# Strassen's scheme in a down projection: more row tile pairs in it, and its sums spread over two engines

## The reference, cut to what matters

```python
h = rms_norm(x, ln_mix_w)
u_pool, q, f, i, g, gate_a, gate_b = split(h @ w_in)             # 2048 x 9216
y_a = multiscale_pool(u_pool) @ w_branch_a                        # 1024 x 2048
y_b = hgrn2(q, f, i, g) @ w_branch_b                              # the recurrence, 1024 x 2048
x = x + (sigmoid(gate_a) * y_a + sigmoid(gate_b) * y_b) @ w_out   # 2048 x 2048
u = conv3(rms_norm(x, ln_ffn_w) @ w_up)                           # 2048 x 11008
x = x + (silu(u_gate) * u_val) @ w_down                           # 5504 x 2048
x = x + sigmoid(rms_norm(x, ln_ple_w) @ w_ple_gate) * (p @ w_ple)
return rms_norm(x, ln_final_w)
```

## Time and profile before

| | us |
|---|---|
| three runs | 1438.47, 1438.48, 4224.24; median 1438.48 |
| the profiled execution's own time | 1438.39 |
| its span in the profile | 1436.6 |
| TensorE busy | 1425.5 (99%), 7112 matmuls |
| VectorE busy | 985.1 (69%) |
| ScalarE busy | 760.0 (53%) |
| GpSimd busy | 216.9 (15%) |
| granted TensorE clock, mean | 0.999 of full |

### The profile page before, as it was taken

How to read it: one execution, slowest core, us unless ns; L and a number is a source line. 1 busy time by engine, 2 the same in 40 slices (tenths; PEclk the granted TensorE clock), 3 DMA queues, 4 the chain that set the end, 5 groups by cost and what they waited for, 6 DMA issues and landing times.

```text
span 1436.6 us, 19705 instructions
## 1 busy us (share of the span) xinstructions
PE 1425.5 (99%) x7112; PEld 1212.1 (84%) x7112; DVE 985.1 (69%) x1180; ACT 760.0 (53%) x920; POOL 216.9 (15%) x153
## 2 busy tenths in 40 slices
PE   9999999999999999999999999999999999999997
PEld 7888888888888888888888888888888888888886
DVE  7576777845455455566777777777777887787755
ACT  7555655544444444555555555555555546554544
POOL 0044144100000000000101101111011531140000
PEclk9999999999999999999999999999999999999999
DMA  9765555456666655465666566565665656565653
GB/s 325 225 205 161 165 176 159 143 194 190 191 190 191 191 190 188 158 208 181 190 188 191 180 198 186 179 204 175 191 193 177 212 192 200 177 213 188 227 200 121
DMA packets 190875, 273.47 MB, mean 190 GB/s; under 512 B 11744, under 2 KB 103136, under 8 KB 190688
## 3 DMA queue, kind: packets, MB, share of 16 engines
q1 hardware_dynamic: 190384, 272.30, 59.6%
q10 hardware_dynamic: 432, 0.37, 0.1%
HBM read 270.53 MB, written 2.10 MB: 190 GB/s over the span
## 4 chain that ended last, share of the span: by engine, by line
PE 98%; DVE 1%; issue 1%; ACT 0%; ACTq 0%; POOLq 0%; POOL 0%; DVEq 0%
PE main L622 15%; PE main L624 15%; PE main L623 15%; PE aux L747 11%; PE main L747 11%; PE aux L756 6%; PE main L756 6%; PE main L672 3%; PE main L670 3%; PE main L671 3%; PE aux L670 3%; PE aux L672 3%; PE aux L671 3%; PE aux L788 1%; PE aux L818 1%
## 5 line engine op out<-in xcount | busy, mean ns | idle before, releaser
L1301 DVE TENSOR_TENSOR w_lo<-raw,w_hi 128x1024 fp32r<-128x1024 f32 (+1 forms) x490 | 612.4, 1260 | 394.5 <-ACT w_hi L1009 394.3
L1009 ACT ACTIVATE w_hi<-raw 128x1024 fp32r<-128x1024 f32 (+1 forms) x490 | 514.1, 1052 | 541.2 <-PE main L624 284.8
L622 PE MATMUL main<-w_hi,xT 128*128 128x512 f32 x702 | 276.8, 394 | 0.0
L624 PE MATMUL main<-w_hi,xT 128*128 128x512 f32 x702 | 273.6, 390 | 0.0
L623 PE MATMUL main<-w_lo,xT 128*128 128x512 f32 x702 | 273.6, 390 | 0.0
L747 PE MATMUL aux<-xT,w_hi 128*128 128x512 f32 x704 | 169.9, 391 | 0.0
L747 PE MATMUL main<-xT,w_hi 128*128 128x512 f32 x672 | 163.0, 391 | 0.0
L624 PEld LDWEIGHTS main<-w_hi,xT 128*128 128x128 f32 x702 | 131.9, 188 | 27.4
L622 PEld LDWEIGHTS main<-w_hi,xT 128*128 128x128 f32 x702 | 132.0, 188 | 27.0 <-issue 0.4
L623 PEld LDWEIGHTS main<-w_lo,xT 128*128 128x128 f32 x702 | 132.0, 188 | 26.1
L747 PEld LDWEIGHTS aux<-xT,w_hi 128*128 128x128 f32 x704 | 129.4, 188 | 25.2 <-issue 0.3
(11 more groups left out here) (270 smaller groups left out, 1770.7 us busy)
## 6 DMA issues: line engine op xcount, KB each, us to landing
raw<-in_w_up SPq DMA_DIRECT2D x336, 256.0 KB
raw<-in_w_in SPq DMA_DIRECT2D x136, 512.0 KB
raw<-in_w_down SPq DMA_DIRECT2D x84, 512.0 KB
raw<-in_w_out SPq DMA_DIRECT2D x32, 512.0 KB
raw<-in_w_ple_gate SPq DMA_DIRECT2D x32, 512.0 KB
raw<-in_w_branch_a SPq DMA_DIRECT2D x16, 512.0 KB
raw<-in_w_branch_b SPq DMA_DIRECT2D x16, 512.0 KB
raw<-in_w_in SPq DMA_DIRECT2D x15, 256.0 KB, 5.7
```

The lines of the kernel that those rows point to most:

```text
L622: pe.matmul(acc, th, wh, start=first, stop=False)
L624: return pe.matmul(acc, tl, wh, start=False, stop=end)
L1009: ac.activation(w_hi[:, u % RING, :, 0:w], raw[:, u % RING, :, 0:w], ACT.Copy).then_inc(hi_full, 1)
L1301: dve.tensor_tensor(w_lo[:, u % RING, :, 0:w], raw[:, u % RING, :, 0:w], w_hi[:, u % RING, :, 0:w].bitcast(F32), ALU.subtract).then_inc(lo ...
```

## The change

More pairs in Strassen's scheme (seven in each half instead of five), the weight sums 2 and 3 on GpSimd instead of VectorE, the four short activation sums on VectorE instead of GpSimd, two buffers for the high and low activation sums, the x transposes of the down stage one unit later with the splits behind them one slot later, and the transpose of the second recurrence output two units later.

```diff
-OBT = [PV[g] + 4 for g in range(2)]
+OBT = [PV[g] + 4 + 2 * g for g in range(2)]
...
-SEVEN_AT = ((5, 8, 11, 14, 17), (5, 8, 11, 14, 17))
+SEVEN_AT = ((5, 7, 9, 11, 13, 15, 17), (5, 7, 9, 11, 13, 15, 17))
...
-X2_AT = {down_slot(n) + 1: n for n in range(NQ)}
+X2_AT = {down_slot(n) + 2: n for n in range(NQ)}
...
-        a_sums_hi = sb("a_sums_hi", [P, 4, P], F32R, ffn)
-        a_sums_lo = sb("a_sums_lo", [P, 4, P], F32R, ffn)
+        a_sums_hi = sb("a_sums_hi", [P, 2, 4, P], F32R, ffn)
+        a_sums_lo = sb("a_sums_lo", [P, 2, 4, P], F32R, ffn)
...
# SyncE, before a load into a buffer of a Strassen pair
-                    sp.wait_ge(w_summed, 3 * (SEVEN[u - RING] + 1))
+                    sp.wait_ge(w_summed, 2 * (SEVEN[u - RING] + 1))
...
# ScalarE, sums_hi
-                    if q:
-                        ac.wait_ge(w_sums_done, 2 * q)
+                    if q > 1:
+                        ac.wait_ge(w_sums_done, 2 * (q - 1))
...
-                    ac.wait_ge(w_summed, 3 * q + (1, 3)[half])
+                    ac.wait_ge(w_summed if half else w_diffs, 2 * (q + 1) if half else q + 1)
...
# ScalarE and VectorE, high and low parts of x after its transposes (norm is 2 in the down stage)
-                        if s == at + 2:
+                        if s == at + 1 + norm:
...
# VectorE, slot u - 2
-            def weight_sums(u):
+            def weight_diffs(u):
                 q, a, b = SEVEN[u], u % RING, u % RING + 1
-                dve.tensor_tensor(w_sums[:, 0:2, :], raw[:, b, 0:2, :], raw[:, a:b + 1, 0, :], ALU.subtract).then_inc(w_summed, 1)
-                dve.wait_ge(w_summed, 3 * q + 1)
-                dve.tensor_tensor(w_sums[:, 2, :], raw[:, b, 1, :], w_sums[:, 0, :], ALU.subtract).then_inc(w_summed, 1)
-                dve.wait_ge(w_summed, 3 * q + 2)
-                dve.tensor_tensor(w_sums[:, 3, :], raw[:, a, 1, :], w_sums[:, 2, :], ALU.subtract).then_inc(w_summed, 1)
+                if q:
+                    dve.wait_ge(w_sums_ready, 2 * q)
+                dve.tensor_tensor(w_sums[:, 0:2, :], raw[:, b, 0:2, :], raw[:, a:b + 1, 0, :], ALU.subtract).then_inc(w_diffs, 1)
+
+            def act_sums(q):
+                dve.wait_ge(a_joined, q + 1)
+                a = a_sums[:].rearrange("p k (b t) -> p k b t", t=P)
+                a11, a12, a21, a22 = a[:, 0, 0], a[:, 1, 0], a[:, 0, 1], a[:, 1, 1]
+                dve.tensor_tensor(a22, a21, a22, ALU.add).then_inc(a_sum_part, 1)
+                dve.wait_ge(a_sum_part, 3 * q + 1)
+                dve.tensor_tensor(a21, a11, a21, ALU.subtract).then_inc(a_sum_part, 1)
+                dve.wait_ge(a_sum_part, 3 * q + 2)
+                dve.tensor_tensor(a11, a22, a11, ALU.subtract).then_inc(a_sum_part, 1)
+                dve.wait_ge(a_sum_part, 3 * q + 3)
+                dve.tensor_tensor(a12, a12, a11, ALU.subtract).then_inc(a_summed, 1)
...
                 if s + 2 in SEVEN:
-                    weight_sums(s + 2)
+                    weight_diffs(s + 2)
+                    act_sums(SEVEN[s + 2])
...
# GpSimd
-            def act_sums(u, q):
+            def join_act(u, q):
                 k = u - DOWN - 2 * UD * (u >= DOWN + 2 * UD)
                 if q == 0:
                     pool.wait_ge(aT_ready, NUP)
                 else:
                     pool.wait_ge(a_sums_ready, q)
                 pool.tensor_tensor(a_sums[:], aT_hi[:, k:k + 2, :].bitcast(F32), aT_lo[:, k:k + 2, :].bitcast(F32),
-                                   ALU.add).then_inc(a_sum_part, 1)
...
+                                   ALU.add).then_inc(a_joined, 1)
+
+            def weight_sums(u, q):
+                a, b = u % RING, u % RING + 1
+                pool.wait_ge(w_diffs, q + 1)
+                pool.tensor_tensor(w_sums[:, 2, :], raw[:, b, 1, :], w_sums[:, 0, :], ALU.subtract).then_inc(w_summed, 1)
+                pool.wait_ge(w_summed, 2 * q + 1)
+                pool.tensor_tensor(w_sums[:, 3, :], raw[:, a, 1, :], w_sums[:, 2, :], ALU.subtract).then_inc(w_summed, 1)
...
             for q, u in enumerate(SEVENS):
-                act_sums(u, q)
+                join_act(u, q)
+                weight_sums(u, q)
```

More of the change, by code:

```diff
@@ L355, in build @@
             sem, ("pT_hi_ready", "pT_ready", "sig_ready", "emb_ready", "y_pre"))
[L357 to L360, removed]
+        w_diffs, w_summed, w_sums_hi_ready, w_sums_ready, w_sums_done = map(
+            sem, ("w_diffs", "w_summed", "w_sums_hi_ready", "w_sums_ready", "w_sums_done"))
+        a_joined, a_sum_part, a_summed, a_sums_hi_ready, a_sums_ready = map(
+            sem, ("a_joined", "a_sum_part", "a_summed", "a_sums_hi_ready", "a_sums_ready"))
         x2_turned, copied, combined = map(sem, ("x2_turned", "copied", "combined"))
@@ L675, in act_block, with act_sum @@
                 return aT_hi[:, k, tb * P:(tb + 1) * P], aT_lo[:, k, tb * P:(tb + 1) * P]
-            def act_sum(k):
-                return a_sums_hi[:, k, :], a_sums_lo[:, k, :]
+            def act_sum(q, k):
+                return a_sums_hi[:, q % 2, k, :], a_sums_lo[:, q % 2, k, :]
             def ring_tile(u, t):
@@ L710, in down_seven @@
                     pe.wait_ge(a_sums_ready, q + 1)
-                    mm = triple(down_acc(2 * p + 1, 0), *act_sum(2), *ring_tile(u, 1), start=False, stop=False)
+                    mm = triple(down_acc(2 * p + 1, 0), *act_sum(q, 2), *ring_tile(u, 1), start=False, stop=False)
                 mm.then_inc(units_done, 1)
@@ L719, in down_sums @@
                 if half == 0:
-                    triple(product(p, 1), *act_sum(3), *sum_tile(0), start=first, stop=end)
-                    mm = triple(product(p, 3), *act_sum(1), *sum_tile(1), start=first, stop=end)
+                    triple(product(p, 1), *act_sum(q, 3), *sum_tile(0), start=first, stop=end)
+                    mm = triple(product(p, 3), *act_sum(q, 1), *sum_tile(1), start=first, stop=end)
                 else:
-                    triple(product(p, 2), *act_sum(0), *sum_tile(2), start=first, stop=end)
+                    triple(product(p, 2), *act_sum(q, 0), *sum_tile(2), start=first, stop=end)
                     mm = triple(down_acc(2 * p, 1), *act_block(2 * i + 1, 1), *sum_tile(3), start=False, stop=False)
@@ L1154, in sums_hi @@
                     ac.wait_ge(a_summed, q + 1)
-                    if q:
-                        ac.wait_ge(w_sums_done, 2 * q)
-                    ac.activation(a_sums_hi[:].rearrange("p k t -> p (k t)"), a_sums[:].rearrange("p k t -> p (k t)"),
+                    if q > 1:
+                        ac.wait_ge(w_sums_done, 2 * (q - 1))
+                    ac.activation(a_sums_hi[:, q % 2].rearrange("p k t -> p (k t)"), a_sums[:].rearrange("p k t -> p (k t)"),
                                   ACT.Copy).then_inc(a_sums_hi_ready, 1)
@@ L1553, in sums_lo @@
                     dve.wait_ge(a_sums_hi_ready, q + 1)
-                    dve.tensor_tensor(a_sums_lo[:].rearrange("p k t -> p (k t)"), a_sums[:].rearrange("p k t -> p (k t)"),
-                                      a_sums_hi[:].rearrange("p k t -> p (k t)").bitcast(F32), ALU.subtract).then_inc(a_sums_ready, 1)
+                    dve.tensor_tensor(a_sums_lo[:, q % 2].rearrange("p k t -> p (k t)"), a_sums[:].rearrange("p k t -> p (k t)"),
+                                      a_sums_hi[:, q % 2].rearrange("p k t -> p (k t)").bitcast(F32), ALU.subtract).then_inc(a_sums_ready, 1)
                 else:
```

11 lines of the change are left out of this document (removed).

## The result

The changed kernel takes 1464.95 us in the median, against 1438.47: ratio of the two 1.018, 95% interval 1.0166 to 1.0194. It is slower, by 26.5 us or 1.8%, clear of the interval but under two per cent. One of the six executions took 2911.72 us and is left out of the ratio, as the one of 4224.24 us before is. The forecast was 1463.5, so 1.4 us are missing from the sum. The profiled execution took 1464.92 us with a span of 1463.1.

The account below looks back on a forecast made before the run. TensorE bounded the kernel; with denser pairs VectorE and GpSimd, taking turns at SBUF, would need 12.5 us per pair against 10.2. 1438.4 - 2.7 - 1.8 + 29.6 = 1463.5 us, range 1440 to 1480.

Parts of the forecast that it names:

- The saving: TensorE, down stage: four more Strassen pairs drop three matmuls each at 0.2267 us, 2.7 us gained.
- the three waits: TensorE waits 0.6 us for x_tok twice and for the recurrence output once; moving steps later gains all 1.8 us.
- The port's load per pair: VectorE and GpSimd take turns into SBUF: 12.5 us together per Strassen pair against TensorE's 10.2.
- the join: GpSimd's 128x512 operation in each Strassen pair, claimed to keep VectorE out of SBUF for 1.12 us.
- What is late first: TensorE's second unit waits for activation sums: 1.0 us at each half's first pair, then 2.3 us at six later pairs.
- The sum: TensorE's lost time over both halves of the down stage: 2 x (1.0 + 6 x 2.3) = 29.6 us.
- the way of the activation sums: From weight differences through short sums, ScalarE and VectorE's low part: some 4.9 us, against 3.6 before.
- The ring of the loads: Weight loads wait until GpSimd's last weight sum has read their buffers: 12.0 us per pair, 10.8 without a low part.
- (b): Rival: GpSimd's work falls into VectorE's idle time, only the wait of loads for buffers costs; 1454 us, chance 0.13.
- (a): Rival: GpSimd is passed over, its second weight sum waiting for two VectorE splits; 1479 us, chance 0.17.
- (c): Rival: not slower, the split running three units ahead takes up the surplus; 1434 us, chance 0.13.
- What would show it: Trace signs: 12 fewer matmuls, TensorE gaps of about 2 us before activation-sum matmuls, GpSimd joins about 12.5 us apart.

Follow-up runs that it names:

- With the short sums first: Changed kernel with VectorE's four short activation sums ahead of the weight differences instead of behind them; 1488.91 us.
- by the columns: Changed kernel with GpSimd's two weight sums over 256 of 512 columns in all pairs but the first; 1449.19 us.
- With the old division: Kernel before with fourteen pairs and the moved steps, weight sums still on VectorE, short sums on GpSimd, one activation-sum buffer; 1452.49 us.
- with memsets and free loads: Changed kernel with GpSimd's weight sums replaced by three memsets and loads waiting only for VectorE's weight differences; 1435.6 us.
- the one with memsets: Changed kernel with GpSimd's two weight sums replaced by three memsets that read nothing, loads still waiting for them; 1456.85 us.
- A long distance behind a short one: Kernel before with moved steps, old work division and twelve pairs, two and three row tile pairs apart in turn; 1442.93 us.
- the loads that don't wait: Changed kernel with GpSimd's weight sums made from weight differences alone and loads waiting only for VectorE's differences; 1463.52 us.

## Why the prediction was right

**The saving.** 12 matmuls fewer, 2.7 us, as counted. The moved steps gain 2.3 us instead of 1.8: the three waits were worth 0.8 us each in the device time, a little over what the profile's column of waits says.

**The port's load per pair.** Forecast 12.5 us, measured 12.55. VectorE's own 9.3 us came out as put. The rest is nearly, but not quite, as put: the two weight sums hold the short sums up by 1.0 us each in the changed kernel and not 1.12, and the join takes up 1.2 us, 0.85 of them VectorE's idle time for ScalarE and 0.38 a split that stands still. The forecast has no wait for ScalarE in this load and 1.12 for the join. That the total is right to 0.05 us is in part luck: the two differences cancel. VectorE's short sum, which no row of before showed, takes 0.28 to 0.29 us at its own pace (0.29 was the middle of the bounds). With the short sums first a weight sum keeps VectorE out for 1.08 us, and by the columns it is 1.11, against 1.12. With the old division the load was put at 11.7 and is 11.85, with memsets and free loads at 10.4 and is 10.52.

**What is late first.** The activation sums are what TensorE waits for, once per pair, as forecast. The first pair costs 1.15 us in each half; 1.0 was taken.

**The sum.** 2 x (1.15 + 6 x 2.35) = 30.5 us lost, less 2.7 and 2.3, gives 25.5; measured 26.5. The forecast had 29.6 - 4.5 = 25.1. In the profiled execution what is missing is covered by the 1.5 us at the lower clock behind the last pair, a term that the forecast doesn't have. Two of its sums are slightly off as written: the ring's terms add up to 11.9 us and not 12.0, and the way of the activation sums to 4.7 and not 4.9; neither moves the total.

**The ring of the loads.** It was named as a second limit right behind the first, 10.8 to 12.0 us. With the port relieved it stands at 12.23 in the mean, a little over the upper end. The statement that the loads don't relieve the port held. Of the rivals, (b) named this very ring and 1454 us; it isn't the changed kernel but nearly the one with memsets, 1456.85.

**The rivals that fell.** (a): GpSimd's three operations take 1.28 to 1.30 us each, so they were not passed over. Even behind a long operation one VectorE operation was all that was waited for. (c): the split three units ahead saved nothing; the activation sums have no such lead. As "What would show it" asked, the joins are 12.5 us apart, TensorE has its gaps before the matmuls that read the activation sums, and the port is free for 0.07 us of a period.

## What to carry to other kernels

Before an engine is relieved, add up the work of both engines that share a port, in the densest stretch and not over the whole kernel: operations of VectorE with two SBUF inputs and operations of GpSimd that read SBUF came one after the other here, so a sum moved from VectorE to GpSimd took 1.1 us of both engines' time where it had taken 0.7. What saves matmuls pays only while the helpers fit into the shorter time: here TensorE saves 0.7 us per pair, and each distance that is one row tile pair too short costs 1.4. And where two rings are nearly equal, undoing either alone shows little; only the two edits together show the size of each.

## What was unexpected

A long distance behind a short one gives nearly nothing back (15.39 us against 15.64), though by the load alone 1.5 us were free. One pair more gained nothing measurable, 1436.2 against 1436.0 us, where 0.7 were due: the trace has them at the new pair itself, in three short waits of which one is VectorE's. And the loads that don't wait, which seemed to gain 1.4 us, gained nothing in the pairs: in the profiled executions the time lay in TensorE's clock, behind the last gap. GpSimd's product in the up stage is still passed over once while the sums of the down stage, in every order tried, never were; no run looked for the reason. The fastest real version of these is the kernel before with the moved steps only, 1436.01 us.
